# A rebuilt first block of a float32 transformer trunk on TensorE: new order, early fetches, other PSUM banks, and 17 matrix products on zeros

## The chip, the cores and the metric

One core of one Trainium2 chip. The metric is the device time of one launch in microseconds; lower is better.

## What is computed

A trunk of two layers over 256 tokens of width 2048, in float32. Layer 0 is sliding-window attention with grouped heads, layer 1 a chunked spatial gating unit, and each is followed by a squared-ReLU MLP of width 8192. The change lies in the very first piece, the keys and values of layer 0:

```python
a = rms_norm(h, g[0])                     # h = x, (1, 256, 2048)
qkv = h @ w_qkv                           # (2048, 2560): 2048 of q, 256 of k, 256 of v
k = qkv[..., Q_WIDTH:Q_WIDTH + KV_WIDTH]; v = qkv[..., Q_WIDTH + KV_WIDTH:]
q = partial_rotary(q, cos, sin); k = partial_rotary(k, cos, sin)
scores = jnp.einsum('bcqkgd,bcjkd->bckgqj', q, kb) * scale
```

## The kernel before

Every large product is cut into blocks of 512 output columns. A block needs 2048 rows of weight, which arrive in eight **slabs** of 512 KB (two times 128 rows). A slab lands in one of four slots of `w_raw`; ScalarE (ACT) rounds it to `w_hi`, and VectorE (DVE) makes `w_lo`, the remainder. TensorE (PE) then makes each float32 product as three: hi by hi, lo by hi, hi by lo (L357 to L359). One slab is six products for token tile 0 and six for token tile 1. `w_hi` and `w_lo` have eight slots each. SyncE (SP) issues the weight transfers in program order; the one into a slot waits until `lo_made` says that the slot's last slab has been split.

The left operand is made in **units**: four 128 x 128 pieces of the residual `h` (one of four column groups, one of two token tiles) are transposed on TensorE (L391), ACT writes `a_hi` from PSUM with the norm's gain (L650), DVE writes `a_lo` (L998). The list `UNIT` sets the order of the units.

Block 0 (`B_KV`) makes keys and values, block 1 (`B_Q`) the first 512 columns of the queries, and 83 more blocks follow. In `first_block(..., first_layer=True)` TensorE works through six slabs for token tile 0, six for tile 1, then the last two for each, with the transpositions of units 2 to 7 between. ACT also squares `h` in four pieces (L669) for the norm. `B_KV`'s results leave PSUM in `kv_evac` (L823, L826). DVE prepares the rotary angles (`rotary_angles`), ACT takes the sine, and DVE rotates the keys (L1209 to L1214). `transpose_k` (L553) on TensorE waits for these keys; it stands in `B_Q` behind 36 of that block's 96 products.

Nothing here is scheduled by a tool: each engine runs its own program in the written order, and semaphores tie them together.

Of the kernel before, what the change touches and what calls it, by code (L numbers as in the profile page):

```python
# [8 lines left out]
F32 = mybir.dt.float32  # L9
F32R = mybir.dt.float32r  # L10
I32 = mybir.dt.int32
ALU = mybir.AluOpType
# [3 lines left out]
P = 128  # L16
# [27 lines left out]
UNITS = len(UNIT)  # L44

# [43 lines left out]
def trunk(nc, x, positions, gains, w_qkv, w_o, sinks, w_in, ln_g, ln_b, w_s, b_s, w_out, w_up, w_down, out):  # L89
    ctx = ExitStack()  # L90
    with ctx:
# [58 lines left out]

        k_sb = yf[:, 0:1024].rearrange("p (t n) -> p t n", t=TOK)
# [23 lines left out]

        x_landed = [sem(f"x_landed{i}") for i in range(UNITS)]
# [7 lines left out]
        consts_made = sem("consts_made")  # L184
        hi_made = sem("hi_made")
# [61 lines left out]

        def slab_ahead(blk, i):

            i = i + 2 * LEAD  # L250
            return (blk, i) if i < 2 * PAIRS else (blk + 1, i - 2 * PAIRS)
# [3 lines left out]
        def _(sp):  # L255
            def load_x(n):
                pair, t = UNIT[n]
                f = slice(pair * COL, (pair + 1) * COL)
                sp.dma_start(h[:, t, f], x[0].rearrange("(t p) n -> p t n", p=P)[:, t, f]).then_inc(x_landed[n], 16)
# [20 lines left out]
            for units, slabs in (([0], (0, 2)), ([1], (2, 3)), ([2, 3], (3, 4)), ([4], (4, 6)), ([5, 6, 7], (6, 8))):  # L280
                for n in units:
                    load_x(n)
                load_block(B_KV, w_qkv[0], D, slabs=range(*slabs))
            with sp.Fori(0, NB) as j:
                load_block(j + B_Q, w_qkv[0], j * COL)
# [56 lines left out]
        def _(pe):  # L342
            def multiply_slab(blk, x_hi, x_lo, i, t):


                if i == 0:

                    at_least(pe, acc_free, blk * 2 + (t - 1))
# [3 lines left out]
                for k in range(SLAB_KB):  # L352
# [4 lines left out]
                    nc.tensor.matmul(acc[t][:, :], lhsT=x_hi[:, kb, tok], rhs=w1, start=(kb == 0), stop=False)  # L357
                    nc.tensor.matmul(acc[t][:, :], lhsT=x_hi[:, kb, tok], rhs=w2, start=False, stop=False)  # L358
                    last = nc.tensor.matmul(acc[t][:, :], lhsT=x_lo[:, kb, tok], rhs=w1,  # L359
# [21 lines left out]
            def transpose_unit(n, use0, first_layer=False):  # L381

                pair, t = UNIT[n]
# [24 lines left out]
            def first_block(blk, use0, first_layer=False):  # L408
# [5 lines left out]
                if first_layer:  # L414
                    transpose_unit(0, use0, True)
                    transpose_unit(1, use0, True)
                for step, (t, i) in enumerate(order):
# [3 lines left out]
                    if step in units:  # L421
                        transpose_unit(units[step], use0, first_layer)
                h_base[0] += 0 if first_layer else UNITS
# [118 lines left out]

            pe.wait_ge(consts_made, 2)
            pe.wait_ge(gains_landed, 16)
            nc.tensor.transpose(sc[0][:, 0:P], gain_rows[:, :], ident[:, :]).then_inc(small_filled, 1)


            first_block(B_KV, 0, first_layer=True)
# [75 lines left out]
        def _(act):  # L624
            def split_slab(blk, i):

                act.wait_ge(slab_landed[i % RAW_SLOTS],
                            blk * (32 * PAIRS // RAW_SLOTS) + 16 * (i // RAW_SLOTS + 1))
                at_least(act, slab_used, blk * (2 * PAIRS) + (i + 1 - SLOTS))
                nc.scalar.activation(w_hi[:, i % SLOTS, :], w_raw[:, i % RAW_SLOTS, :], ACT.Copy).then_inc(hi_made, 1)  # L630

            def split_slabs(blk, pair):
                for i in (2 * pair, 2 * pair + 1):
                    split_slab(blk, i)
# [9 lines left out]
            def split_unit(n, use0, norm):  # L644

                pair, t = UNIT[n]
# [18 lines left out]

            def square_h(t, part):
# [5 lines left out]
            def first_block(blk, use0, norm, evac, layer0=False):  # L672
# [3 lines left out]
                h_seen[0] += 0 if layer0 else UNITS  # L676

                def square(t, part):
                    if layer0:
                        for pair in (2 * part, 2 * part + 1):  # L680
                            act.wait_ge(x_landed[UNIT.index((pair, t))], 16)
                    else:

                        act.wait_ge(h_ready, h0 + UNIT.index((2 * part + 1, t)) + 1)
                    square_h(t, part)

                if layer0:
                    split_unit(0, use0, norm)
                    split_slabs(0, 0)
                    split_unit(1, use0, norm)  # L690
                    split_slabs(0, 1)
                split_unit(2, use0, norm)
                if layer0:
                    split_slabs(0, 2)
                else:
                    split_ahead(blk - 1, 3)
                split_unit(3, use0, norm)
                if layer0:
                    split_ahead(blk, 0)
                split_unit(4, use0, norm)  # L700
                if not layer0:
                    split_next(blk, 0)
                square(0, 0)
                split_unit(5, use0, norm)
                split_next(blk, 2 if layer0 else 1)
                square(1, 0)
                split_unit(6, use0, norm)
                split_next(blk, 3 if layer0 else 2)
# [3 lines left out]
                if not layer0:  # L712
                    split_next(blk, 3)
# [43 lines left out]
            def mlp(base, layer, use0, n, then):  # L757
# [42 lines left out]
                with act.Fori(1, QUARTERS - 1) as q:  # L800
# [8 lines left out]
            act.dma_start(pos_i[:, :], positions[0].rearrange("(t p) -> p t", p=P),  # L809
                          allow_slow_non_contiguous=True).then_inc(pos_landed, 16)  # L810
            for i in range(2):
                act.dma_start(sink_rows[i * CHUNK:(i + 1) * CHUNK, :, :],
                              sinks[0].rearrange("(a i e) -> i a e", i=2, e=2)[i].partition_broadcast(CHUNK),
                              allow_slow_non_contiguous=True).then_inc(sinks_landed, 16)
            act.wait_ge(small_filled, 1)
            nc.scalar.activation(gain_cols[:, :], sc[0][:, 0:P], ACT.Copy).then_inc(small_copied, 1)
# [3 lines left out]
            def kv_evac(t):  # L820
                product_done(act, B_KV, t)
                once = acc[t][:, 0:256].rearrange("p (g d) -> p g d", g=KVH)
# [3 lines left out]
                nc.scalar.activation(v_band[:, 2 * t, :], acc[t][:, 256:512], ACT.Copy, scale=r_in[:, t:t + 1]  # L826
                                     ).then_inc(acc_free, 1)

            first_block(B_KV, 0, 0, kv_evac, layer0=True)
# [139 lines left out]
        def _(dve):  # L969
# [4 lines left out]
            def split_slab(blk, i):  # L974

                dve.wait_ge(hi_made, blk * (2 * PAIRS) + (i + 1))
                nc.vector.tensor_tensor(w_lo[:, i % SLOTS, :], w_raw[:, i % RAW_SLOTS, :],  # L977
                                        w_hi[:, i % SLOTS, :].bitcast(F32), ALU.subtract).then_inc(lo_made, 1)

            def split_slabs(blk, pair):  # L980
                for i in (2 * pair, 2 * pair + 1):
                    split_slab(blk, i)
# [9 lines left out]
            def split_unit(n, use0, norm):  # L992
                pair, t = UNIT[n]
# [34 lines left out]
            def first_block(blk, use0, norm, layer0=False):  # L1028

                def update(n):  # L1030
                    if not layer0:
                        update_h(n)

                if layer0:
                    split_unit(0, use0, norm)
                    split_slabs(0, 0)
                    split_unit(1, use0, norm)
                    split_slabs(0, 1)
                split_unit(2, use0, norm)
                if layer0:  # L1040
                    split_slabs(0, 2)
                else:
                    split_ahead(blk - 1, 3)
                update(4)
                split_unit(3, use0, norm)
                if layer0:
                    split_ahead(blk, 0)
                update(5)
# [364 lines left out]
```

## Time and profile before

| | before |
|---|---|
| median of three runs | 1971.51 us (1971.41 to 1972.63) |
| profiled execution, its span | 1971.5 us |
| PE busy | 1949.2 us (99%) |
| DVE busy | 1076.2 us (55%) |
| ACT busy | 972.2 us (49%) |
| HBM read | 365.51 MB |

The span runs from the first to the last instruction; no time of the profiled execution is known beside it, so span and time are the same number here. Busy time is the sum of an engine's instructions without overlap. "PE" is a matrix product or a transposition, "PEld" its weight load.

### The profile page before, as it was taken

How to read it: one execution, taken by the hardware profiler on the slowest of the kernel's cores; microseconds unless marked ns; L12 is line 12 of the kernel's file. 1: busy time of each engine (PE TensorE's matmuls, PEld its weight loads, DVE VectorE, ACT ScalarE, POOL GpSimd, SP SyncE). 2: the span in 40 equal slices, each digit the busy share in tenths (PEclk: the TensorE clock that was granted, in tenths of full speed). 3: DMA queues.
4: the chain of work that ended last, by engine and by line, in shares of the span. 5: the costliest groups of instructions: out<-in, count | busy, mean ns of one | idle time of the engine just before them, and what ended most of it. 6: DMA issues, size and time to landing. Idle time of an engine off the chain costs nothing.

```text
span 1971.5 us, 26643 instructions
## 1 busy us (share of the span) xinstructions
PE 1949.2 (99%) x8914; PEld 1604.2 (81%) x8914; DVE 1076.2 (55%) x1276; ACT 972.2 (49%) x1339; POOL 6.2 (0%) x23
## 2 busy tenths in 40 slices
PE   7999999999999999999999999999999999999998
PEld 5777888888888888888888888888888888888886
DVE  5666575454454455455667655654544554544455
ACT  6666465435434543454564445654355435434542
POOL 0000000000000000000000000000000000000000
PEclk9999999999999999999999999999999999999999
DMA  6634656555555555555475555565555555555553
GB/s 205 203 128 164 207 197 203 191 192 182 191 195 180 189 192 192 192 172 196 150 259 171 192 189 177 173 212 199 194 177 188 196 191 190 178 199 189 182 192 107
DMA packets 189833, 368.40 MB, mean 187 GB/s; under 512 B 12616, under 2 KB 12752, under 8 KB 189008
## 3 DMA queue, kind: packets, MB, share of 16 engines
q1 hardware_dynamic: 187264, 360.75, 54.8%
q0 software_dynamic: 1040, 6.82, 0.9%
q8 instruction: 34, 0.56, 0.1%
q10 hardware_dynamic: 1472, 0.08, 0.0%
q14 instruction: 23, 0.19, 0.0%
HBM read 365.51 MB, written 2.10 MB: 186 GB/s over the span
## 4 chain that ended last, share of the span: by engine, by line
PE 98%; DMA 1%; ACT 0%; DVE 0%; SPq 0%; issue 0%; DVEq 0%; ACTq 0%
PE acc L357 31%; PE acc L359 31%; PE acc L358 31%; PE t L378 2%; DMA w_raw<-in_attn_w_qkv 1%; PE t L391 1%; PE scores L459 0%; PE o L481 0%; PE t L469 0%; PE scores L591 0%; PE t L439 0%; ACT a_hi L650 0%; DVE w_lo L977 0%; DVE h L1014 0%; ACT w_hi L630 0%
## 5 line engine op out<-in xcount | busy, mean ns | idle before, releaser
L977 DVE TENSOR_TENSOR w_lo<-w_raw,w_hi 128x1024 fp32r<-128x1024 f32 x680 | 820.6, 1224 | 632.1 <-ACT w_hi L630 603.5
L630 ACT ACTIVATE w_hi<-w_raw 128x1024 fp32r<-128x1024 f32 x680 | 708.4, 1058 | 626.0 <-PE acc L359 590.9
L357 PE MATMUL acc<-w_hi,a_hi 128*128 128x512 f32 x1440 | 573.5, 398 | 4.8 <-DVE w_lo L977 4.4
L359 PE MATMUL acc<-w_hi,a_lo 128*128 128x512 f32 x1440 | 563.2, 391 | 0.0
L358 PE MATMUL acc<-w_lo,a_hi 128*128 128x512 f32 x1440 | 562.5, 391 | 0.0
L357 PE MATMUL acc<-w_hi,b_hi 128*128 128x512 f32 x1280 | 500.9, 391 | 0.0
L359 PE MATMUL acc<-w_hi,b_lo 128*128 128x512 f32 x1280 | 498.4, 389 | 0.0
L358 PE MATMUL acc<-w_lo,b_hi 128*128 128x512 f32 x1280 | 498.1, 389 | 0.0
L357 PEld LDWEIGHTS acc<-w_hi,a_hi 128*128 128x128 f32 x1440 | 271.3, 188 | 62.2 <-issue 7.5
L359 PEld LDWEIGHTS acc<-w_hi,a_lo 128*128 128x128 f32 x1440 | 271.2, 188 | 58.3
L358 PEld LDWEIGHTS acc<-w_lo,a_hi 128*128 128x128 f32 x1440 | 271.6, 189 | 53.5
L357 PEld LDWEIGHTS acc<-w_hi,b_hi 128*128 128x128 f32 x1280 | 240.3, 188 | 50.3 <-issue 0.8
L359 PEld LDWEIGHTS acc<-w_hi,b_lo 128*128 128x128 f32 x1280 | 240.3, 188 | 50.3
L358 PEld LDWEIGHTS acc<-w_lo,b_hi 128*128 128x128 f32 x1280 | 240.4, 188 | 49.1
L726 ACT ACTIVATE s<-acc,r_in 128x512 f32<-128x512 f32 x80 | 55.1, 689 | 116.5 <-PE acc L359 115.8
L656 ACT ACTIVATE b_hi<-t 128x512 f32 (+1 forms) x72 | 42.9, 599 | 92.6 <-PE t L378 92.2
L1006 DVE TENSOR_TENSOR b_lo<-t,b_hi 128x512 f32 (+1 forms) x72 | 49.4, 688 | 65.6 <-ACT b_hi L656 65.6
L1075 DVE TENSOR_TENSOR y<-acc,y 128x512 f32 (+1 forms) x48 | 33.2, 691 | 69.7 <-PE acc L359 69.7
L733 ACT ACTIVATE o<-y 128x512 f32<-128x512 f32 (+1 forms) x32 | 19.3, 602 | 87.1 <-DVE y L1075 50.0
L998 DVE SCALAR_TENSOR_TENSOR a_lo<-t,gain_cols,a_hi 128x128 fp32r<-128x128 f32 x128 | 36.0, 344 | 21.8 <-ACT a_hi L650 21.4
L650 ACT ACTIVATE a_hi<-t,gain_cols 128x128 fp32r<-128x128 f32 x128 | 36.5, 370 | 19.6 <-PE t L391 18.8
L1077 DVE COPY y<-acc 128x512 f32 (+1 forms) x32 | 22.1, 691 | 41.0 <-PE acc L359 40.9
(120 smaller groups left out, 475.6 us busy)
## 6 DMA issues: line engine op xcount, KB each, us to landing
w_raw<-in_mlp_w_up SPq DMA_DIRECT2D x256, 512.0 KB, 4.2
w_raw<-in_mlp_w_down SPq DMA_DIRECT2D x256, 512.0 KB, 4.4
w_raw<-in_sgu_w_in SPq DMA_DIRECT2D x64, 512.0 KB, 4.6
w_raw<-in_attn_w_qkv SPq DMA_DIRECT2D x40, 512.0 KB, 4.6
w_raw<-in_attn_w_o SPq DMA_DIRECT2D x32, 512.0 KB, 4.2
w_raw<-in_sgu_w_out SPq DMA_DIRECT2D x32, 512.0 KB, 4.4
gain<-in_norm_gains POOLq DMA_DIRECT2D x4, 1024.0 KB, 5.4
h<-in_x SPq DMA_DIRECT2D x8, 256.0 KB, 11.4
```

The lines of the kernel that those rows point to most:

```text
L357: nc.tensor.matmul(acc[t][:, :], lhsT=x_hi[:, kb, tok], rhs=w1, start=(kb == 0), stop=False)
L358: nc.tensor.matmul(acc[t][:, :], lhsT=x_hi[:, kb, tok], rhs=w2, start=False, stop=False)
L359: last = nc.tensor.matmul(acc[t][:, :], lhsT=x_lo[:, kb, tok], rhs=w1, start=False, stop=(kb == KB - 1))
L378: last = nc.tensor.transpose(tb[t][:, k * P:(k + 1) * P], s[:, t, k * P:(k + 1) * P], ident[:, :])
L630: nc.scalar.activation(w_hi[:, i % SLOTS, :], w_raw[:, i % RAW_SLOTS, :], ACT.Copy).then_inc(hi_made, 1)
L650: last = nc.scalar.activation(a_hi[:, kb, t * P:(t + 1) * P], tb[n % 2][:, k * P:(k + 1) * P], ACT.Copy, scale=gain_cols[:, norm * KB + kb ...
L656: nc.scalar.activation(b_hi[:, bass.ds(kb0, 4), t * P:(t + 1) * P], tb[t][:, :].rearrange("p (k n) -> p k n", k=4), ACT.Copy).then_inc(t_h ...
L726: return nc.scalar.activation(dst, acc[t][:, :], func, scale=r_in[:, t:t + 1])
L977: nc.vector.tensor_tensor(w_lo[:, i % SLOTS, :], w_raw[:, i % RAW_SLOTS, :], w_hi[:, i % SLOTS, :].bitcast(F32), ALU.subtract).then_inc(lo ...
L998: nc.vector.scalar_tensor_tensor(out=a_lo[:, kb, tok], in0=tb[n % 2][:, k * P:(k + 1) * P], scalar=gain_cols[:, norm * KB + kb:norm * KB + ...
L1006: nc.vector.tensor_tensor(b_lo[at], tb[t][:, :].rearrange("p (k n) -> p k n", k=4), b_hi[at].bitcast(F32), ALU.subtract).then_inc(t_lo, 4)
L1075: nc.vector.tensor_tensor(dst, acc[t][:, :], dst, ALU.add).then_inc(acc_free, 1)
```

## The change

1. **Order of the transfers.** SP issues a unit of `x` and a slab in turn, eight of each (`X_UNIT` order: column group by column group, both token tiles). Slabs 4 to 7 of `B_KV` land in `y`, which is unused until then (`kv_raw`), so that none of the sixteen transfers waits for a slot. The first four slabs of `B_Q` are queued behind them, each behind the split of a `B_KV` slab.
2. **Order of the products.** `kv_block` replaces `first_block` for `B_KV`: two slabs for token tile 0, the same two for tile 1, then the next two. ACT and DVE split unit i and slab i in turn, then `B_Q`'s slabs.
3. **Banks.** `B_KV` accumulates in the two banks of `scores`, not in `acc`, so `B_Q` starts without waiting for `kv_evac`.
4. **Products on zeros.** DVE zeroes a part of `b_hi`; TensorE multiplies it 17 times into the bank `o1`, which nothing reads: five of 512 columns first of all, four of 256 after unit 0, four of 512 and four of 256 after unit 1.
5. **Small transfers.** The positions and the sinks (ACT's queue, rows of 4 and 8 bytes) are issued behind the eighth split instead of at the start. `neg_sink` moves behind the rotation of the first queries.

```diff
+X_UNIT = [(pair, t) for pair in range(NB) for t in range(TOK)]
+        kv_raw = yf[:, :].rearrange("p (i n) -> p i n", i=RAW_SLOTS)
-            for units, slabs in (([0], (0, 2)), ([1], (2, 3)), ([2, 3], (3, 4)), ([4], (4, 6)), ([5, 6, 7], (6, 8))):
...
+            for i in range(2 * PAIRS):
+                load_x(i)
+                sp.dma_start(raw(B_KV, i).rearrange("p (k n) -> p k n", k=SLAB_KB), kv_source(i)
+                             ).then_inc(slab_landed[i] if i < RAW_SLOTS else kv_landed[i - RAW_SLOTS], 16)
+            for i in range(RAW_SLOTS):
+                sp.wait_ge(lo_made, i + 1)
...
-                if i == 0:
-
-                    at_least(pe, acc_free, blk * 2 + (t - 1))
+                if i == 0 and not (isinstance(blk, int) and blk <= B_Q):
+
+                    pe.wait_ge(acc_free, blk * 2 + (t - 1))
...
+            def idle_products(count, n):
+
+                zeros = b_hi[:, 0:2, :].rearrange("p k n -> p (k n)")
+                for _ in range(count):
+                    nc.tensor.matmul(ob[1][:, 0:n], lhsT=zeros[:, 0:P], rhs=zeros[:, 0:n], start=True, stop=True)
+
+            def kv_block():
+
+                transpose_unit(0, 0, True)
+                idle_products(4, SEQ)
+                transpose_unit(1, 0, True)
+                idle_products(4, SEQ * TOK)
+                idle_products(4, SEQ)
+                for pair in range(PAIRS):
+                    for t in range(TOK):
+                        for i in (2 * pair, 2 * pair + 1):
+                            pe.wait_ge(t_lo, X_UNIT.index((pair, t)) * 4 + (i % 2 + 1) * SLAB_KB)
+                            multiply_slab(B_KV, a_hi, a_lo, i, t, sc)
+                            if pair < PAIRS - 1 and (t, i % 2) in ((0, 1), (1, 0)):
+                                transpose_unit(2 * pair + 2 + t, 0, True)
...
+            pe.wait_ge(zeros_made, 1)
+            idle_products(5, SEQ * TOK)
             pe.wait_ge(consts_made, 2)
             pe.wait_ge(gains_landed, 16)
...
+            def kv_block(evac):
+
+                squares = {3: (0, 0), 4: (1, 0), 6: (0, 1), 7: (1, 1)}
+                for i in range(2 * PAIRS):
+                    split_unit(i, 0, 0, X_UNIT)
+                    split_slab(B_KV, i)
+                    if i in squares:
+                        t, part = squares[i]
+                        for pair in (2 * part, 2 * part + 1):
+                            act.wait_ge(x_landed[X_UNIT.index((pair, t))], 16)
+                        square_h(t, part)
+                load_positions()
+                load_sinks()
+                split_next(B_KV, 2, 3, 4)
+                take_root()
+                split_next(B_KV, 5)
+                act.wait_ge(norm_done, norms[0])
+                evac(0)
+                evac(1)
+                split_next(B_KV, 6, 7)
...
+            def kv_block():
+
+                for i in range(2 * PAIRS):
+                    split_unit(i, 0, 0, X_UNIT)
+                    split_slab(B_KV, i)
+                split_next(B_KV, 2, 3)
+                input_norm()
+                split_next(B_KV, 4, 5)
+                rotary_angles()
+                split_next(B_KV, 6, 7)
...
+            nc.vector.memset(b_hi[:, 0:2, :].bitcast(F32), 0.0).then_inc(zeros_made, 1)
```

`split_next(B_KV, i)` splits the slab six ahead, so `split_next(B_KV, 2)` is the first slab of `B_Q`, and 3 to 7 are its slabs 1 to 5.

On TensorE the program began, before the change, with the transposition of the gains, then units 0 and 1 and at once the products:

```order
L545 MATMUL scores<-ident,gain_rows 128x128 [waits gains_landed,consts_made]
L391 MATMUL t<-ident,h 128x128 [waits x_landed0]
...
L391 MATMUL t<-ident,h 128x128 [waits x_landed1]
...
L357 MATMUL acc<-w_hi,a_hi 128x512 [waits lo_made,t_lo]
L358 MATMUL acc<-w_lo,a_hi 128x512
```

It now begins so (`o` is the bank that nothing reads):

```order
L431 MATMUL o<-b_hi 128x512 [waits zeros_made]
L431 MATMUL o<-b_hi 128x512 x4
L584 MATMUL o<-ident,gain_rows 128x128 [waits gains_landed,consts_made]
L410 MATMUL t<-ident,h 128x128 [waits x_landed0]
L410 MATMUL t<-ident,h 128x128 x3
L431 MATMUL o<-b_hi 128x256 x4
L410 MATMUL t<-ident,h 128x128 [waits x_landed1]
L410 MATMUL t<-ident,h 128x128 x3
L431 MATMUL o<-b_hi 128x512 x4
L431 MATMUL o<-b_hi 128x256 x4
L376 MATMUL scores<-w_hi,a_hi 128x512 [waits lo_made,t_lo]
```

The products on zeros stand around the first two units, ahead of the first real product.

On ACT, at the end of the unit splits (`a_hi`), the order before was this, with two of `B_Q`'s slabs split between the squares (`b_hi,pre_ssq`), and the positions and sinks long issued:

```order
L630 ACTIVATE w_hi<-w_raw 128x1024 [waits slab_used,slab_landed1]
L669 ACTIVATE b_hi,pre_ssq<-h 128x1024 [waits x_landed6,x_landed2]
...
L669 ACTIVATE b_hi,pre_ssq<-h 128x1024 [waits x_landed7,x_landed5]
L662 ACTIVATE root<-mean_sq 128x2 [waits norm_mean]
L823 ACTIVATE y<-acc,r_in 128x512 [waits half_done,norm_done]
L826 ACTIVATE work<-acc,r_in 128x256
L630 ACTIVATE w_hi<-w_raw 128x1024 [waits slab_used,slab_landed2]
```

And now, from the last slab of `B_KV` (which comes out of `y`) on:

```order
L675 ACTIVATE w_hi<-y 128x1024
L720 ACTIVATE b_hi,pre_ssq<-h 128x1024
L708 DMA pos_i<-in_positions 128x2x1
L713 DMA sink_rows<-in_attn_sinks 64x8x2 x2
L675 ACTIVATE w_hi<-w_raw 128x1024 x3
L703 ACTIVATE root<-mean_sq 128x2
L675 ACTIVATE w_hi<-w_raw 128x1024
L872 ACTIVATE y<-scores,r_in 128x512
L875 ACTIVATE work<-scores,r_in 128x256
```

The three small transfers and all of `B_Q`'s splits now stand behind the last square.

On DVE the rotary angles (`pos_f` to `red`) stood ahead of `B_Q`'s slabs 2 to 5 (`w_lo` x4), and then came the rotation of the keys:

```order
L1026 RECIPROCAL r_in<-root 128x2
L1176 CAST pos_f<-pos_i 128x2
...
L1192 TENSOR_SCALAR red<-red 128x16
L1193 TENSOR_SCALAR red<-red 128x32
L1196 TENSOR_SCALAR neg_sink<-sink_rows 128x16
L977 TENSOR_TENSOR w_lo<-w_raw,w_hi 128x1024 x4
L1209 TENSOR_TENSOR rot<-y,sincos 128x128
```

Now two of these slabs stand between the norm and the angles, and two between the angles and the rotation:

```order
L1077 TENSOR_TENSOR sum_sq<-pre_ssq 128x2 [waits norm_sum]
...
L1071 RECIPROCAL r_in<-root 128x2 [waits norm_root]
L1026 TENSOR_TENSOR w_lo<-w_raw,w_hi 128x1024 [waits hi_made] x2
L1218 CAST pos_f<-pos_i 128x2 [waits consts_made,pos_landed]
...
L1235 TENSOR_SCALAR red<-red 128x32 [waits dve_chain]
L1026 TENSOR_TENSOR w_lo<-w_raw,w_hi 128x1024 [waits hi_made] x2
L1249 TENSOR_TENSOR rot<-y,sincos 128x128 [waits qkv_evac,sincos_made]
```

## Rows read from the trace of the kernel before

**Rows 1.** Windows, 566 to 1166 us: busy us (and instructions) of each engine, clock, DMA share, GB/s.

```profile
566.00:1166.00 600.00, 599.74 (x2709) 496.00 (x2709) 333.23 (x365) 285.99 (x349) 1.98 (x3) 1.00 0.57 189
```

**Rows 2.** Timeline, 0 to 11 us: start, duration, engine, and idle time with its end.

```profile
1.52 0.45 ACTq L809 DMA_DIRECT2D pos_i<-in_positions  x1
...
2.74 0.73 ACTq L812 DMA_DIRECT2D sink_rows<-in_attn_sinks  x1
...
4.39 1.06 PE L391 MATMUL t<-ident,h 128*128 128x128 f32 x4
...
5.56 1.14 ACT L650 ACTIVATE a_hi<-t,gain_cols 128x128 fp32r<-128x128 f32 x4 [0.64 <-PE t L391]
...
7.86 1.22 DVE L977 TENSOR_TENSOR w_lo<-w_raw,w_hi 128x1024 fp32r<-128x1024 f32 x1
...
10.46 1.11 PE L391 MATMUL t<-ident,h 128*128 128x128 f32 x4 [5.01 <-DMA h<-in_x]
```

**Rows 3.** DMA, 8 to 12, 20 to 24, 16 to 20 us: packets, MB, share; time to landing.

```profile
q1 hardware_dynamic: 384, 0.73, 53.8%
q10 hardware_dynamic: 391, 0.00, 4.5%
...
q1 hardware_dynamic: 786, 1.46, 95.6%
...
w_raw<-in_attn_w_qkv SPq DMA_DIRECT2D x1, 512.0 KB, 9.6
```

**Rows 4.** Timeline at two gaps of TensorE; windows, one microsecond in the second gap.

```profile
14.89 0.66 PE L391 MATMUL t<-ident,h 128*128 128x128 f32 x4 [0.76 <-DMA h<-in_x]
...
23.16 0.77 PE L357 MATMUL acc<-w_hi,a_hi 128*128 128x512 f32 x1 [4.40 <-DVE w_lo L977]
...
22.00:23.00 1.00, 0.00 (x0) 0.00 (x0) 1.00 (x2) 1.00 (x5) 0.00 (x0) 0.50 1.04 393
```

**Rows 5.** Timeline, one unit and one slab on their way through three engines.

```profile
31.54 0.60 PE L391 MATMUL t<-ident,h 128*128 128x128 f32 x4
...
32.17 1.14 ACT L650 ACTIVATE a_hi<-t,gain_cols 128x128 fp32r<-128x128 f32 x4 [0.66 <-PE t L391]
...
33.19 1.07 ACT L630 ACTIVATE w_hi<-w_raw 128x1024 fp32r<-128x1024 f32 x1
...
33.35 1.13 DVE L998 SCALAR_TENSOR_TENSOR a_lo<-t,gain_cols,a_hi 128x128 fp32r<-128x128 f32 x4 [1.60 <-ACT a_hi L650]
...
34.14 1.07 ACT L669 ACTIVATE b_hi<-h 128x1024 fp32r<-128x1024 f32 x1
...
34.39 1.22 DVE L977 TENSOR_TENSOR w_lo<-w_raw,w_hi 128x1024 fp32r<-128x1024 f32 x1
...
34.75 0.60 PE L391 MATMUL t<-ident,h 128*128 128x128 f32 x4
...
35.38 0.88 ACT L650 ACTIVATE a_hi<-t,gain_cols 128x128 fp32r<-128x128 f32 x3
```

**Rows 6.** Timeline, 40 to 54 us: norm, angles, rotation, and the transposition of the keys.

```profile
40.80 0.15 DVE L1063 TENSOR_TENSOR sum_sq<-pre_ssq 128x2 f32<-128x2 f32 x1
...
41.51 0.17 DVE L1176 CAST pos_f<-pos_i 128x2 f32<-128x2 int32 x1
...
43.19 0.39 PE L357 MATMUL acc<-w_hi,a_hi 128*128 128x512 f32 x1
...
43.93 0.18 DVE L1193 TENSOR_SCALAR red<-red 128x32 f32<-128x32 f32 x1
...
50.13 0.29 DVE L1209 TENSOR_TENSOR rot<-y,sincos 128x128 f32<-128x128 f32 x1
...
51.27 0.28 DVE L1214 TENSOR_TENSOR y<-rot 128x128 f32<-128x128 f32 x1
...
53.16 0.39 PE L359 MATMUL acc<-w_hi,a_lo 128*128 128x512 f32 x1
53.40 0.60 PE L553 MATMUL t<-ident,y 128*128 128x128 f32 x4
```

More of the change, by code:

```diff
@@ L173, in trunk @@
         junk = ob[1]
+        kv_landed = [sem(f"kv_landed{i}") for i in range(RAW_SLOTS)]
         x_landed = [sem(f"x_landed{i}") for i in range(UNITS)]
@@ L256, in load_x @@
             def load_x(n):
-                pair, t = UNIT[n]
+                pair, t = X_UNIT[n]
                 f = slice(pair * COL, (pair + 1) * COL)
@@ L277, in load_mlp, with kv_source @@
                             load_block(q * (2 * NB) + j + (base + NB), w_down[layer], j * COL, q * KB)
-            for units, slabs in (([0], (0, 2)), ([1], (2, 3)), ([2, 3], (3, 4)), ([4], (4, 6)), ([5, 6, 7], (6, 8))):
[L281 to L284, printed above, removed]
+            def kv_source(i):
+                rows = w_qkv[0].rearrange("(k p) n -> p k n", p=P)
+                return rows[:, i * SLAB_KB:(i + 1) * SLAB_KB, D:D + COL]
+            for i in range(2 * PAIRS):
[4 more added lines that the diff above has]
+                sp.wait_ge(lo_made, i + 1)
+                src = w_qkv[0].rearrange("(k p) n -> p k n", p=P)[:, i * SLAB_KB:(i + 1) * SLAB_KB, 0:COL]
+                sp.dma_start(w_raw[:, i, :].rearrange("p (k n) -> p k n", k=SLAB_KB), src).then_inc(slab_landed[i], 16)
+            load_block(B_Q, w_qkv[0], 0, slabs=range(RAW_SLOTS, 2 * PAIRS))
+            with sp.Fori(1, NB) as j:
                 load_block(j + B_Q, w_qkv[0], j * COL)
@@ L642, in split_ahead, with split_unit @@
                 split_next(blk, 2 * pair, 2 * pair + 1)
-            def split_unit(n, use0, norm):
-                pair, t = UNIT[n]
+            def split_unit(n, use0, norm, order=UNIT):
+                pair, t = order[n]
                 act.wait_ge(t_filled, use0 + n + 1)
@@ L664, in _, with load_positions, load_sinks @@
             norms = [0]
+            def load_positions():
+                act.dma_start(pos_i[:, :], positions[0].rearrange("(t p) -> p t", p=P),
+                              allow_slow_non_contiguous=True).then_inc(pos_landed, 16)
+            def load_sinks():
+                for i in range(2):
+                    act.dma_start(sink_rows[i * CHUNK:(i + 1) * CHUNK, :, :],
+                                  sinks[0].rearrange("(a i e) -> i a e", i=2, e=2)[i].partition_broadcast(CHUNK),
+                                  allow_slow_non_contiguous=True).then_inc(sinks_landed, 16)
             def square_h(t, part):
@@ L675, in first_block @@
+            def first_block(blk, use0, norm, evac):
                 h0 = h_seen[0]
-                h_seen[0] += 0 if layer0 else UNITS
+                h_seen[0] += UNITS
                 def square(t, part):
[L679 to L684, printed above, removed]
-                    square_h(t, part)
@@ L808, in _ @@
             nc.scalar.activation(warm[:, :], ident[:, 0:1], ACT.Sqrt)
[L809 to L814, printed above, removed]
             act.wait_ge(small_filled, 1)
-            nc.scalar.activation(gain_cols[:, :], sc[0][:, 0:P], ACT.Copy).then_inc(small_copied, 1)
+            nc.scalar.activation(gain_cols[:, :], ob[0][:, 0:P], ACT.Copy).then_inc(small_copied, 1)
             act.wait_ge(small_copied, 1)
@@ L990, in split_ahead, with split_unit @@
                 split_next(blk, 2 * pair, 2 * pair + 1)
-            def split_unit(n, use0, norm):
-                pair, t = UNIT[n]
+            def split_unit(n, use0, norm, order=UNIT):
+                pair, t = order[n]
                 dve.wait_ge(t_hi, use0 + n + 1)
```

136 lines of the change are left out of this document (55 added, 81 removed).

## The prediction

> **What bounds the kernel.** I read the page first (PE busy for 99% of the span, DVE for 55%, ACT for 49%), then the busy time by stretch: in the middle of the program PE is busy for 599.74 of 600 us [rows 1]. TensorE's waits lie at the two ends, most of them in the first 24 us, and there I read the timeline. So TensorE sets the time, and a change of the first block is worth exactly what it moves a TensorE instruction behind which nothing waits any more. The best such mark is the transposition of the keys, `transpose_k`: it starts at 53.40 us, 0.24 us behind the product ahead of it, without a wait [rows 6]. The program behind it does not change. My measure of the change is therefore when `transpose_k` starts.
>
> Three things are lost before it. TensorE waits 5.01 us for `x`; the second unit's transposition starts at 10.46 us [rows 2]. From 18.76 to 23.16, 4.40 us, it waits for the split of slab 3, and in this wait the granted clock falls to 0.50, which is 1.2 GHz [rows 4]. The products behind it run at that level for about five microseconds.
>
> The cause of the late `x` and slab 3 is in the DMA queues. From 8 to 12 us queue q1 (x and weights) moves 384 packets, and q10 (gains, positions, sinks) 391 packets that hold next to nothing; from 20 to 24 us, with q10 all but empty, q1 moves 786 [rows 3]. The sum is the same, about 195 packets a microsecond: a packet of 4 bytes takes the turn of one of 2 KB. While they are under way the weights get half of the rate, 183 instead of 366 GB/s.
>
> **The early fetches.** A unit of `x` is 128 packets, a slab 256. The second unit now stands behind 384 packets, plus 128 of the gains: 640 in all, at 195 a microsecond 3.3 us, from about 2.3 us on. With 0.5 to 1 us until the last has landed that is 6.1 to 6.6 us, not 10.46. All sixteen transfers are 3072 packets, 16 us, so slab 7 has landed by about 19 us. The recurrence below asks for it at 34 us: the DMA leaves the path.
>
> **The new block as a chain.** What it costs comes from one unit and slab on their way through the engines [rows 5]. From the start of a transposition it is 0.63 us to `a_hi`, 1.18 more to `a_lo`, 1.04 more to `w_lo`, 1.22 until that is done, and 0.14 to the product: 4.21 us. Products follow each other at (53.16 - 43.19)/44 = 0.2266 us [rows 6], so six are 1.36. Transpositions of two units are 3.21 us apart with twelve products between [rows 5]; that leaves 0.49 us for a transposition.
>
> In `kv_block` the unit of the next pair is transposed behind the second slab of token tile 0. Until the next pair's first slab is needed TensorE has 2 x (0.49 + 1.36) = 3.70 us of work, but the chain takes 4.21: it waits 0.5. The second slab's `w_lo` comes 2.2 us after the first's (DVE does a slab, 1.14, then a unit, 1.04), and TensorE has six products, 1.36, to fill this: it waits 0.85. A pair takes 4.21 + 2.2 + 1.36 = 7.8 us instead of the 6.4 of its work. A square on ACT takes 1.24 us (34.14 to 35.38) [rows 5]. The one at i = 3 falls in a gap of ACT. Those at i = 4 and i = 6 stand between the slab and the next unit and push the second `w_lo` back by 1.0 us.
>
> Start: DVE's first `w_lo` begins at 7.86 us as before [rows 2]; then unit 1, and `w_lo` of slab 1 ends at 7.86 + 1.14 + 1.04 + 1.22 = 11.26. That needs unit 1 transposed from 6.6 us on, which the landing above just gives. Products of slab 1 start at 11.4, the transposition of unit 2 at 12.8, of unit 4 at 12.8 + 7.8 = 20.6, of unit 6 at 20.6 + 8.8 = 29.4. The block ends 4.21 + 2.2 + 1.0 us and eighteen products (4.08) later: **40.9 us**. Before it ended 36 products ahead of 53.40, at 45.2. So the block alone gives 4.3 us.
>
> **What is late next.** The splits of `B_Q` and the keys' rotation. ACT ends slab 7 at 29.4 + 5.8 = 35.2 us and the last square at 36.4. Then come the three small DMA issues, as long as before: from 1.52 to 3.47, 1.95 us [rows 2]. So `B_Q`'s slab 0 is rounded from 38.4 us on, where before ACT had two of these slabs done before 38. DVE then works without a pause: slabs 0 and 1 end at 41.9, the norm takes 0.8 (from `sum_sq` at 40.80 to 41.59) [rows 6], slabs 2 and 3 end at 45.0, the angles take 2.6 (41.51 to 44.11) [rows 6] to 47.6, slabs 4 and 5 end at 50.0, and the rotation takes 1.42 (50.13 to 51.55) [rows 6] to 51.4. ACT is beside this, not ahead: `kv_evac` of tile 1 ends by 45.3, slabs 4 and 5 by 47.6, table and sine by 49.2.
>
> TensorE would reach `transpose_k` at 40.9 + 36 x 0.2266 = 49.0 us. The keys are rotated at 51.4, so it starts at **51.5** and waits 2.5 us. Against 53.40 that is 1.9 us gained; 2.4 of the 4.3 are given back. Of the 1.9 nothing is lost later: ACT and DVE are half idle in the rest [rows 1].
>
> **Edits at no cost.** Products on zeros: five of 512 columns at 1.2 GHz are 2.1 us and end at about 3.5 us, before the gains' transposition (right ahead of unit 0, which starts at 4.39) [rows 2]. The eight between unit 1 and the first product end by 10.1 us even at 1.2 GHz, and the chain asks for slab 1 at 11.4; six real products lie between, so at worst TensorE is 0.1 to 1.2 us late. The zeroing itself is one DVE instruction in an idle stretch. Bound from below: nothing; from above, with the clock at 1.2 GHz until 12 us, 1.0 us. I take nothing, since the longer activity should have raised the clock by 9 us: before, the engine was at work without a long pause from 10.46 us on [rows 2], and at 14.89 a transposition takes 0.66 us instead of 1.11 [rows 4]. The other banks: `B_Q` would wait for `kv_evac` of tile 0 (44.2 us in the new order), so without them the block's gain would be gone; with them it costs nothing. `neg_sink` is 0.17 us of DVE.
>
> **The small transfers** now meet `B_Q`'s slabs 4 to 7. They are issued at 36.4 to 38.4 us; `B_Q`'s slabs 4 and 5 are requested when slabs 0 and 1 are split, 40.8 and 42.0. Those 512 packets at half of the rate [rows 3] take 5.2 us, and land at about 47.7. DVE can't use slab 5 before 48.8, so ACT must have it by 47.6. Cost: 0 to 0.2 us; if the rate is three quarters of this, 1.9 us. I add 0.1, and forecast 1971.5 - 1.9 + 0.1 = 1969.7 us. The profiled span equals the median of the runs (1971.51), so it needs no correction.
>
> **Rivals.** 0.2% (3.9 us) is about what a measurement of this kernel can tell from no change.
> - *`transpose_k` is not late (16%).* If the ACT and DVE chain is 2.5 us shorter than I make it, for instance since squares and splits overlap better, the whole 4.3 us stay: 1967.2, and up to 1966.5 with faster pairs. For it: ACT and DVE are not full in the rows. Against it: DVE has no gap from 39.5 to 51.4 us in my sum.
> - *The small packets hold `B_Q` up (12%), slower.* Slab 5 lands late. Each microsecond of its landing past 47.6 is one at `transpose_k`; past 49.5 the kernel is slower than before. A landing 9.6 us after the request (a slab took this before, beside such packets [rows 3]) gives 51.6, `transpose_k` at 55.4, and 1973.5.
> - *The clock stays low (9%), slower.* The block now waits at every pair, up to 1.9 us at a time. With all its products at 0.427 us (1.2 GHz) the chain becomes product bound and `transpose_k` moves to about 58.5: 1976.6. Before, the wait of 4.40 us cost the clock, and one of 0.76 us did not [rows 4]; 1.9 lies between. By the Trainium skill, "TensorE: Matmul & The Clock Gate", section "HAM oscillation — how this bites in real kernels", a kernel whose bursts are short beside its DMA waits falls back to the low clock at every tile; taken for this block that is the 1976.6. In the trace above the shorter wait speaks against it.
> - *It does little (6%).* If `x` lands at 9 us, because the rate and not the order was the limit, all is 1.9 to 2.4 us later: 1971.5 to 1972.
>
> **Chances.** My forecast, `transpose_k` between 50.5 and 52.8 us, 57%. Its own range is 1968.6 to 1971.0. The range for 8 in 10 takes in the first rival and the middle of the second: 1966.9 to 1973.5. Faster by over 0.2%: the first rival and a corner of the forecast, 17%. Slower: the clock and the far end of the packets, 10%. Within: 73%.
>
> **What would show it.** Unit 1's transposition at 6.1 to 6.6 us; unit 2's at 12.8, unit 4's at 20.6, unit 6's at 29.4; TensorE idle 0.5 and 0.9 us in the second pair, 0.5 and 1.9 in the third and fourth; granted clock 1.00 from 9 us on. `B_KV`'s last product near 40.9; a wait of about 2.5 us of the keys' transposition for DVE, starting at 51.5; q1 at some 98 packets a microsecond while q10 runs, now from 38 to 50 us. Wrong would be: a low clock behind 12 us, ACT waiting for a `B_Q` slab past 48 us, or a new wait of TensorE behind 55 us.

## The result and the profile after

The changed kernel takes 1974.64 us (median of 20 runs, 1972.83 to 1976.51), the kernel before 1972.05 us (20 runs, 1971.1 to 1973.09). The ratio is 1.0013, with a 95% interval of 1.0007 to 1.0019: **2.6 us slower**, where 1969.7 was forecast. The time lies outside the range. The difference is small, 0.13%, but its interval does not reach zero, and it goes the other way than I forecast.

The chain of the rebuilt block came out as worked out; what follows it did not. TensorE's timeline of the changed kernel (start, duration, and the idle time ahead with its end) has the forecast marks 12.8, 20.6 and 29.4 at 12.84, 20.67 and 29.37. `B_Q` starts at 40.80:

```profile
1.47 2.50 PE L431 MATMUL o<-b_hi 128*128 128x512 f32 x5 [1.47 <-DVE b_hi L1239]
...
6.60 0.66 PE L410 MATMUL t<-ident,h 128*128 128x128 f32 x4 [0.31 <-DMA h<-in_x]
...
12.84 0.60 PE L410 MATMUL t<-ident,h 128*128 128x128 f32 x4
...
20.67 0.60 PE L410 MATMUL t<-ident,h 128*128 128x128 f32 x4
...
27.90 0.47 PE L376 MATMUL scores<-w_hi,a_hi 128*128 128x512 f32 x1 [1.38 <-DVE w_lo L1026]
...
29.37 0.60 PE L410 MATMUL t<-ident,h 128*128 128x128 f32 x4
...
40.80 0.39 PE L376 MATMUL acc<-w_hi,a_hi 128*128 128x512 f32 x1
...
52.88 0.66 PE L592 MATMUL t<-ident,y 128*128 128x128 f32 x4 [3.76 <-DVE y L1254]
...
57.71 0.60 PE L592 MATMUL t<-ident,y 128*128 128x128 f32 x4
```

Against [rows 6]: `transpose_k` starts at 52.88 instead of 53.40, behind a wait of 3.76 us where there was none. Its two halves are 4.83 us apart; in the kernel before they are 3.2. Each of the two has a cause of its own.

The first is seen on ACT, in its timeline (an ACTq line is the issue of a transfer). It rounds `B_Q`'s slabs 0 to 2 from 35.99 us on and is done with `kv_evac` by 42.8. Then it stands still:

```profile
31.96 0.39 ACTq L708 DMA_DIRECT2D pos_i<-in_positions  x1
...
33.11 0.65 ACTq L713 DMA_DIRECT2D sink_rows<-in_attn_sinks  x1
...
34.96 1.10 ACT L720 ACTIVATE b_hi<-h 128x1024 fp32r<-128x1024 f32 x1
...
35.99 2.99 ACT L675 ACTIVATE w_hi<-w_raw 128x1024 fp32r<-128x1024 f32 x3
...
47.48 1.06 ACT L675 ACTIVATE w_hi<-w_raw 128x1024 fp32r<-128x1024 f32 x1 [4.65 <-DMA w_raw<-in_attn_w_qkv]
48.76 1.06 ACT L675 ACTIVATE w_hi<-w_raw 128x1024 fp32r<-128x1024 f32 x1 [0.23 <-DMA w_raw<-in_attn_w_qkv]
...
51.13 0.23 ACT L882 ACTIVATE sincos<-red 128x32 f32<-128x32 f32 x1
```

The two at 47.48 and 48.76 us are `B_Q`'s slabs 4 and 5, requested from 38.4 us on. The DMA view from 36 to 40 us (first two lines) and from 40 to 44 shows what the queues did meanwhile: packets, MB, share, then time to landing.

```profile
q10 hardware_dynamic: 441, 0.00, 4.9%
...
w_raw<-in_attn_w_qkv SPq DMA_DIRECT2D x2, 512.0 KB, 9.2
...
q1 hardware_dynamic: 57, 0.12, 8.4%
q10 hardware_dynamic: 322, 0.00, 3.6%
```

The small packets went at 110 a microsecond although they had the DMA engines to themselves (which were busy for 4.9% of the time), and they did not share: the weights requested at 38.4 us moved no packet before 43 us and 57 until 44 us. The two slabs took 9.2 us.

The second cause is the clock. The windows view (busy us of PE, PEld, DVE, ACT and POOL, then PEclk, DMA share, GB/s) shows it at full level when the wait ends at 52.88 us, at half from 55 us on at the latest, and back by 58 us:

```profile
52.00:53.00 1.00, 0.12 (x1) 0.12 (x2) 0.96 (x5) 1.00 (x2) 0.00 (x0) 1.00 1.01 391
...
55.00:56.00 1.00, 1.00 (x4) 0.81 (x3) 0.92 (x4) 0.08 (x1) 0.00 (x0) 0.50 0.69 121
...
58.00:59.00 1.00, 1.00 (x7) 0.87 (x6) 0.24 (x1) 0.60 (x1) 0.00 (x0) 1.00 1.03 373
```

### The profile page after: what moved, and what is told of

The parts are those of the page before. It is cut to its first block, busy times and chain, and to the rows that moved or that the text cites. A ratio compares the mean times of both kernels' runs of the same rounds, so it can differ in the third digit from the quotient of the medians.

```text
span 1972.5 us, 26652 instructions
## 1 busy us (share of the span) xinstructions
PE 1953.3 (99%) x8931; PEld 1605.5 (81%) x8931; DVE 1075.9 (55%) x1277; ACT 971.5 (49%) x1339; POOL 6.2 (0%) x23
## 4 chain that ended last, share of the span: by engine, by line
PE 97%; DVE 1%; ACT 1%; DMA 1%; issue 0%; ACTq 0%; DVEq 0%
PE acc L376 31%; PE acc L378 31%; PE acc L377 31%; PE t L397 2%; PE t L410 1%; ACT a_hi L691 1%; PE scores L496 0%; DVE w_lo L1026 0%; DMA w_raw<-in_attn_w_qkv 0%; PE o L518 0%; DVE a_lo L1043 0%; PE t L506 0%; PE scores L630 0%; ACT b_hi L720 0%; ACT w_hi L675 0%
## 5 line engine op out<-in xcount | busy, mean ns | idle before, releaser
L376 PE MATMUL acc<-w_hi,a_hi 128*128 128x512 f32 x1408 | 559.5, 397 | 0.4 <-ACT y L781 0.2
L378 PE MATMUL acc<-w_hi,a_lo 128*128 128x512 f32 x1408 | 549.9, 391 | 0.0
L377 PE MATMUL acc<-w_lo,a_hi 128*128 128x512 f32 x1408 | 549.2, 390 | 0.0
L378 PEld LDWEIGHTS acc<-w_hi,a_lo 128*128 128x128 f32 x1408 | 264.7, 188 | 56.7
L376 PEld LDWEIGHTS acc<-w_hi,a_hi 128*128 128x128 f32 x1408 | 264.7, 188 | 56.5 <-issue 2.9
L377 PEld LDWEIGHTS acc<-w_lo,a_hi 128*128 128x128 f32 x1408 | 265.1, 188 | 52.4
```

The lines of the kernel that those rows point to most:

```text
L376: nc.tensor.matmul(bank[t][:, :], lhsT=x_hi[:, kb, tok], rhs=w1, start=(kb == 0), stop=False)
L377: nc.tensor.matmul(bank[t][:, :], lhsT=x_hi[:, kb, tok], rhs=w2, start=False, stop=False)
L378: last = nc.tensor.matmul(bank[t][:, :], lhsT=x_lo[:, kb, tok], rhs=w1, start=False, stop=(kb == KB - 1))
```

## The experiments

Each kernel was run beside the kernel before on the same chip. Ratios are to it. The kernel before has medians of 1971.98 to 1972.72 us in these rounds, so a difference between two kernels of different rounds is good to some tenths of a microsecond; the marks of the profiled runs stand beside it. Twelve kernels:

| kernel | median us | ratio (95%) | `transpose_k` at |
|---|---|---|---|
| e0_before | 1972.63 | 1.0002 (0.9993 to 1.0011) | 52.7 |
| e1_small_in_gap | 1968.90 | 0.9983 (0.9974 to 0.9992) | 49.55 |
| e2_fill_wait | 1973.03 | 1.0005 (0.9996 to 1.0014) | 53.16 |
| e3_sink_rows | 1969.02 | 0.9985 (0.9976 to 0.9994) | 48.90 |
| e4_before_sink_rows | 1964.82 | 0.9964 (0.9950 to 0.9978) | 44.98 |
| e5_no_zeros | 1971.00 | 0.9994 (0.9985 to 1.0004) | 49.91 |
| e6_acc_banks | 1970.31 | 0.9990 (0.9981 to 0.9999) | 50.5 |
| e7_slot_waits | 1969.08 | 0.9986 (0.9977 to 0.9995) | 48.77 |
| e8_best | 1964.71 | 0.9960 (0.9946 to 0.9973) | 45.54 |
| e9_units_early | 1963.46 | 0.9955 (0.9942 to 0.9969) | 43.4 |
| e10_x_early | 1964.54 | 0.9960 (0.9947 to 0.9974) | 44.7 |
| e11_units_small | 1969.95 | 0.9988 (0.9979 to 0.9997) | 48.90 |

### The yardstick

e0_before is the kernel before.

> The kernel before once more, unchanged, as a yardstick: its span beside its time, and its spread. The changed kernel's profiled span is 1.0 us above that of before (1972.5 against 1971.5), but its median time is 2.6 us above. Theory A (what lies outside the span is the same for both): the span here varies and is near 1970.2 us, with the time 1.8 us above it, as for the changed kernel. Theory B (the change also costs time outside the span): span 1971.5, time within 0.6 us of it.

Its profiled execution took 1972.63 us with a span of 1970.8, and in all its runs the time is the span and 1.8 us; so it is for the changed kernel (1974.34 and 1972.5). Theory A holds. By the same 1.8 us, the span of 1971.5 that the prediction started from belongs to one of that kernel's longer executions, of about 1973.3 us.

### The small packets: elsewhere, or fewer

e1_small_in_gap issues them behind slab 4:

```diff
                         square_h(t, part)
-                load_positions()
-                load_sinks()
+                    if i == 4:
+                        load_positions()
+                        load_sinks()
```

> The changed kernel, with positions and sinks issued behind the split of slab 4 (near 22 us) instead of behind slab 7; their 1280 small packets at 110 a microsecond then end by 36 us, before B_Q's slab 4 is requested at 38.4. Theory M (the packets hold the weights back): slab 4 lands in 4.6 us, not 9.2, the keys are rotated at 48.8, transpose_k starts at 49.0 without a wait, the clock stays up; 5.5 us less than the changed kernel, 3 to 4.4 us less than before. Rival R (ACT's and DVE's own order is what makes the keys late): transpose_k still at 51.5 or later with a wait of 2.5 us or more; at most 1.5 us less than the changed kernel. Rival R2: the small packets now hold back B_Q's slabs 0 to 3, and ACT waits for slab 0 past 36 us.

e3_sink_rows fetches the whole row of 32 sinks to every partition, and DVE picks:

```diff
-                for i in range(2):
-                    act.dma_start(sink_rows[i * CHUNK:(i + 1) * CHUNK, :, :],
-                                  sinks[0].rearrange("(a i e) -> i a e", i=2, e=2)[i].partition_broadcast(CHUNK), ...)
+                act.dma_start(sink_rows[:, :, :, :].rearrange("p a i e -> p (a i e)"),
+                              sinks[0].partition_broadcast(P)).then_inc(sinks_landed, 16)
```

> The changed kernel, with the sinks fetched as 128 rows of 128 bytes instead of 1024 pieces of 8 bytes, and one more small DVE instruction to pick each half's entries; place of issue unchanged. Theory M (the number of packets counts): the small transfers end by 36 us, transpose_k starts at 49.0 without a wait, 5.5 us less than the changed kernel. Rival R (ACT's and DVE's order): transpose_k at 51.5 or later. Rival R3 (the place among the weights counts, not the number): slab 4 still lands 9 us after its request.

In both, the wait of `transpose_k` is gone, and the time is 5.7 and 5.6 us under the changed kernel's 1974.64. The lines of e3_sink_rows that answer to those above are, first from its DMA view (36 to 40 us):

```profile
w_raw<-in_attn_w_qkv SPq DMA_DIRECT2D x2, 512.0 KB, 4.1
```

and from its timeline, ACT's two lines and TensorE's one:

```profile
42.67 1.07 ACT L675 ACTIVATE w_hi<-w_raw 128x1024 fp32r<-128x1024 f32 x1
44.13 1.06 ACT L675 ACTIVATE w_hi<-w_raw 128x1024 fp32r<-128x1024 f32 x1 [0.39 <-DMA w_raw<-in_attn_w_qkv]
...
48.90 0.60 PE L592 MATMUL t<-ident,y 128*128 128x128 f32 x4
```

The same two slabs now take 4.1 us, and the keys are ready in time. Theory M holds: the sinks' 1024 pieces held the weights back. (The new fetch has fewer pieces and longer ones, 16 KB in all instead of 8, so these two runs do not tell the number from the length.) Rival R (DVE's and ACT's order), which was a step of my prediction, falls. R3 falls too, since the place of issue was the same. R2 did not come about: in e1 ACT rounds `B_Q`'s slab 0 from 36.58 us without a wait. For e1 the mark is 0.5 us later than expected: its whole block runs 0.6 us late from the start.

### The clock alone

e2_fill_wait puts 16 unread products into the wait.

```diff
-            plain_block(B_Q, a_hi, a_lo, {(1, 0): [lambda: transpose_k(0)], ...
+            plain_block(B_Q, a_hi, a_lo, {(1, 0): [lambda: idle_products(16, SEQ * TOK), lambda: transpose_k(0)], ...
```

> The changed kernel, with 16 more unread products of 512 columns right ahead of transpose_k, where TensorE waits 3.8 us. Theory M: transpose_k stays at 52.9 us, but the granted clock stays 1.00, the two groups of key transpositions are 3.2 us apart instead of 4.8, and the kernel is 1.6 us faster than the changed one (about 1 us slower than before). Rival (the clock falls for another reason, such as the low activity since 16 us): it falls all the same, and nothing is won or 16 products at 0.427 us make transpose_k later.

TensorE's timeline of this kernel:

```profile
49.22 3.79 PE L431 MATMUL o<-b_hi 128*128 128x512 f32 x16
53.16 0.66 PE L592 MATMUL t<-ident,y 128*128 128x128 f32 x4
...
56.41 0.60 PE L592 MATMUL t<-ident,y 128*128 128x128 f32 x4
```

The granted clock stays 1.00, the halves are 3.25 us apart, and the kernel is 1.6 us under the changed one (1974.64 - 1973.03). The wait itself made the clock fall, and that is 1.6 us of the loss. With the 4.0 us at `transpose_k` (52.88 against 48.90 in e3) it makes up the 5.6 us between the changed kernel and e3.

### The old block with the same small fix

e4_before_sink_rows is the kernel before with the sinks' fetch of e3 and nothing else.

> The kernel before, with nothing changed but the fetch of the sinks: 128 rows of 128 bytes instead of 1024 pieces of 8 bytes, and one more small DVE instruction. Theory M (the small packets, not the order of the old block, made x and slab 3 late): the small packets end by about 7 us, slab 3 lands near 14 us instead of 20.6, the 4.4 us wait and the low clock behind it go, and transpose_k starts 3 to 6 us earlier than in the kernel before: at least 0.15% less than before, as good as the rebuilt block. Rival (the rebuilt order is what brings the gain): less than 1 us gained.

It is 0.36% faster than the kernel before and beats every version with the change's own order of units. TensorE's timeline, to be held against [rows 2, 4, 6]:

```profile
9.21 1.12 PE L391 MATMUL t<-ident,h 128*128 128x128 f32 x4 [3.68 <-DMA h<-in_x]
...
16.71 0.60 PE L391 MATMUL t<-ident,h 128*128 128x128 f32 x4
...
19.93 0.60 PE L391 MATMUL t<-ident,h 128*128 128x128 f32 x4
...
23.14 0.60 PE L391 MATMUL t<-ident,h 128*128 128x128 f32 x4
...
44.98 0.60 PE L553 MATMUL t<-ident,y 128*128 128x128 f32 x4
```

Behind 9.21 us TensorE waits for nothing until 60 us, and from 16.71 us on the units are 3.2 us apart, which is twelve products and a transposition. From 8 to 12 us q1 moves 845 packets here, against 384 in [rows 3]. The old order was good; its fetch of the sinks was not. And this is what the rebuilt block is worth by itself: with the sinks as rows in both kernels it is 4.2 us slower than the old one (1969.02 against 1964.82, `transpose_k` at 48.90 against 44.98). It waits for `w_lo` at every pair, 4.5 us in all from 12 us on, where the old block does not wait.

### The other parts of the change, each on e3_sink_rows

e5_no_zeros leaves out the 17 products on zeros:

```diff
                 transpose_unit(0, 0, True)
-                idle_products(4, SEQ)
                 transpose_unit(1, 0, True)
-                idle_products(4, SEQ * TOK)
-                idle_products(4, SEQ)
...
-            idle_products(5, SEQ * TOK)
```

> The changed kernel with the sinks as rows (e3_sink_rows), without the 17 products on zeros. If they hold the clock up: the products from 9.2 us on run at 1.2 GHz for some microseconds, the two first slabs take 2.56 us each instead of 1.4, unit 2's transposition starts 1.0 to 1.5 us later than 12.8, and all behind it too: 1.0 to 1.5 us slower than e3_sink_rows. Rival (the wait for slab 1's split covers it, or the clock would be up anyway): within 0.3 us of e3_sink_rows.

```profile
9.29 0.76 PE L376 MATMUL scores<-w_hi,a_hi 128*128 128x512 f32 x1 [1.44 <-DVE w_lo L1020]
9.85 0.63 PE L377 MATMUL scores<-w_lo,a_hi 128*128 128x512 f32 x1
...
12.83 0.39 PE L378 MATMUL scores<-w_hi,a_lo 128*128 128x512 f32 x1
```

In its profiled execution the first products, from 9.29 us, are about 0.43 us apart until 12.8, which is the pace of 1.2 GHz, and `transpose_k` is 1.0 us later. (PEclk reads 1.00 in these microseconds; so early in the program the pace has to be read.) The median is 2.0 us above e3. The zeros are worth 1 to 2 us.

e6_acc_banks takes the banks `acc` again:

```diff
-                            multiply_slab(B_KV, a_hi, a_lo, i, t, sc)
+                            multiply_slab(B_KV, a_hi, a_lo, i, t)
```

> The changed kernel with the sinks as rows, with B_KV accumulated in the banks acc again, so that B_Q's first product waits for kv_evac of tile 0, which ends near 41.8 us, where TensorE is ready at 40.7. Theory (the banks are worth this wait): TensorE waits 1.1 us there, transpose_k at 50.0 instead of 48.9, 1.1 us slower than e3_sink_rows. Rival (evacuation is on time): no difference.

```profile
42.21 0.50 PE L376 MATMUL acc<-w_hi,a_hi 128*128 128x512 f32 x1 [0.97 <-ACT work L873]
```

This row of its timeline is `B_Q`'s first product: it waits 0.97 us for the evacuation. The kernel is 1.3 us slower than e3.

e7_slot_waits makes SP wait for the split of slab i - 4 ahead of slab i:

```diff
                 load_x(i)
+                if i >= RAW_SLOTS:
+                    sp.wait_ge(lo_made, i - RAW_SLOTS + 1)
```

> The changed kernel with the sinks as rows, where SP waits for the split of slab i - 4 before it issues slab i of B_KV, as it would with four slots only. Theory (the early fetch of slabs 4 to 7 is worth nothing once the queue is free and the order is right): slab 4 is requested near 9 us, slab 7 near 19 and needed at 34, no wait moves, within 0.3 us of e3_sink_rows. Rival (the early fetches carry the gain): TensorE waits for slabs 4 to 7, over 1 us slower than e3_sink_rows.

It takes 1969.08 us, 0.06 us from e3: fetching slabs 4 to 7 early, into `y`, is worth nothing once the queue is free.

### The chain inside the block

e9_units_early, again on e3_sink_rows, transposes each unit one group of six products earlier:

```diff
-                            if pair < PAIRS - 1 and (t, i % 2) in ((0, 1), (1, 0)):
-                                transpose_unit(2 * pair + 2 + t, 0, True)
+                            if pair < PAIRS - 1 and t == 0:
+                                transpose_unit(2 * pair + 2 + i % 2, 0, True)
```

> The changed kernel with the sinks as rows, with both units of the next column group transposed one product group earlier (behind slab 2p and slab 2p+1 of token tile 0). Theory C (the chain unit, a_hi, a_lo, w_lo paces the rebuilt block: TensorE waits for it 0.4 to 1.4 us per slab, 4.5 us in all from 12 us on): the waits shrink by 1.4 us each, the block ends about 3 us earlier, transpose_k near 46, 3 us less than e3_sink_rows. Rival (ACT and DVE are full, so earlier units only make them finish the slabs in another order): less than 1 us.

The waits view shows what TensorE waited for `w_lo` until 60 us, in the changed kernel (first line) and in this one:

```profile
PE scores L376 <- DVE w_lo L1026: 5.6, 8, 1.4
```

```profile
PE scores L376 <- DVE w_lo L1024: 0.6, 3, 0.2
```

Theory C holds, and the gain was underestimated: 5.6 us (1969.02 - 1963.46) instead of 3. I had taken only the shift of a transposition; in fact the chain no longer adds up from pair to pair. This is the fastest kernel, 0.45% under the kernel before.

e10_x_early and e8_best go on from e4. In e10 the second unit of `x` is requested ahead of slab 1, since e4 still waits 3.68 us for it; e8 has the 17 products on zeros besides.

```diff
-            for units, slabs in (([0], (0, 2)), ([1], (2, 3)), ...
+            for units, slabs in (([0], (0, 1)), ([1], (1, 3)), ...
```

> The kernel before with the sinks as rows (e4_before_sink_rows), with the second unit of x moved ahead of slab 1 in SP's order. Theory: unit 1 lands near 6.7 us instead of 9.2, the first products start when w_lo of slab 0 is ready, near 9.2 instead of 10.1, and the rest follows: 0.5 to 1 us less than e4_before_sink_rows. Rival: slab 2 and 3 then set the pace, no difference.

> As e10_x_early, plus the 17 products on zeros of the change. If clock and fetch order add up: all real products at 2.4 GHz from 9.2 us on, 1 to 2.5 us less than e4_before_sink_rows (1962.3 to 1963.8 against a kernel before of 1972), the fastest version so far. Rival: DVE's splits of slabs 2 and 3 take over as the bound, at most 0.5 us less than e10_x_early.

Neither gains what was expected. e10 (1964.54, five runs, 1964.38 to 1964.95) overlaps with e4 (1964.56 to 1965.19). Its first product starts 0.5 us earlier and its fourth unit 1.0 us (15.68 against 16.71), but `transpose_k` only 0.3 us. It waits 1.42 us for slab 0's `w_lo`, as expected, and 0.51 us at 18.17 us for slab 4's. Ahead of that one ACT had waited 1.03 us for slab 3 to land, which fits the rival in part; it is not tested. In e8's profiled execution TensorE gets `x` only at 8.68 us, and the zeros leave a gap of 2.34 us. The clock falls at about 10 us, 1.3 us behind the gap's end, with the products on zeros running (the last line is of the windows view):

```profile
8.68 0.66 PE L392 MATMUL t<-ident,h 128*128 128x128 f32 x4 [2.34 <-DMA h<-in_x]
...
11.01 0.63 PE L358 MATMUL acc<-w_hi,a_hi 128*128 128x512 f32 x1
...
10.00:11.00 1.00, 1.00 (x6) 0.90 (x5) 0.00 (x0) 0.67 (x1) 0.00 (x0) 0.52 1.06 408
```

### A second case for the packets

e11_units_small is e9's order with the change's own small transfers.

> The changed kernel with the units transposed earlier (as in e9_units_early) but with its own small transfers, 1280 packets, issued now near 27 us. A test of the packet account on a case it was not made from: 1280 packets at 110 a microsecond end near 39 us; B_Q's slabs 4 and 5, requested near 33 and 34, land near 41 and 42.3, about 9 us after their request; sine, rotation, and transpose_k at 46.2 to 46.8, where e9_units_early has it at 43.4; TensorE waits about 3 us and the clock may fall behind it. 3 to 5 us slower than e9_units_early, 6 us less than the changed kernel. Rival (the packets only delay what the rebuilt chain had made late anyway): within 1 us of e9_units_early.

```profile
48.90 1.11 PE L592 MATMUL t<-ident,y 128*128 128x128 f32 x4 [5.25 <-DVE y L1254]
```

The direction holds, the rival (within 1 us of e9) falls, and the size is above the forecast: slab 4 is rounded from 43.50 us on, not 41, and `transpose_k` waits 5.25 us. Behind that wait the clock is low, and the two halves are 5.13 us apart. The kernel is 6.5 us slower than e9. It is 4.7 us, not 6, under the changed one. The block now ends earlier, so the transfers are issued earlier too (26.95 instead of 31.96), but the slabs are asked for 5.5 us earlier too (32.90 instead of 38.37). A faster block only waits longer for the same packets.

## Why the prediction was wrong

- **The chain of the block: right.** Four marks within 0.1 us, and unit 1 was transposed from 6.60 us; the 0.5 to 1 us that its forecast allowed for the landing stood in no row.
- **"What is late next": wrong in its cause.** I made DVE and ACT the bound of the rotation (51.4 us) and put the three DMA issues on ACT's path with 1.95 us. They did not stand there: they were issued from 31.96 us on, 3.0 us before the square began that stands ahead of them in the program (34.96), and `B_Q`'s slab 0 began at 35.99 instead of 38.4. With the packets gone the keys were ready at 48.5 and nothing waited (e3). So my first rival, `transpose_k` not late, was the truth about ACT and DVE.
- **"The small transfers": the step that failed.** My sum has them at 0.1 us; they cost 4.0 us at `transpose_k` and, through the clock, 1.6 more. I let the weights take half of the rate beside the small packets and landed slab 5 at about 47.7, although requested as late as 42.0. The [rows 3] count, 384 against 391, shows sharing between transfers that had all been requested by then. It does not say what a weight requested behind 1280 small packets gets. It got nothing until they were nearly done, and alone they ran at 110 a microsecond, not 195. Nor was it the time of the DMA engines that the small packets took: in [rows 3] the two queues had them busy for 53.8% and 4.5%. Slab 5 was taken at 48.8. That is my second rival, at 1.2 us past its bound of 47.6. That `transpose_k` came only 1.3 us behind its forecast (52.88 against 51.6) is luck: without the packets ACT and DVE let it start at 48.90 (e3), 2.6 us earlier than the 51.5 I made it, and that hid most of the 4.0 us.
- **The clock: the rival's mechanism, in another place.** The waits in the block, up to 1.39 us, did not lower the clock. The wait that the packets made did: 1.6 us (e2). I had priced the two rivals apart, and one was the cause of the other. By the Trainium skill, "TensorE: Matmul & The Clock Gate", section "HAM oscillation — how this bites in real kernels", a long enough DMA wait between bursts of products drops the clock, so that the next burst starts slow. This trace agrees in part: behind the one long wait (3.76 us) PEclk is 0.50 from 55 us on, but still 1.00 in the first microsecond of products. That the short waits at every pair would do the same was my reading, and they did not.
- **"The profiled span equals the median, so it needs no correction": wrong.** The time is 1.8 us above the span in every run. The starting point, 53.40 and 1971.5, was one of the longer executions; another had `transpose_k` at 52.74 and 1970.8. From there to the changed kernel's 1972.5 is 1.7 us: 0.1 at `transpose_k` and 1.6 of clock. So the 4.6 us between my 1969.7 and the profiled execution's 1974.34 are 1.8 of this, 1.3 at `transpose_k` and 1.6 of clock, to 0.1 us. The first is an error of the starting number alone; the direction was wrong by the other two.
- **The zeros and the banks.** Zeros at no cost: right; e5 shows what they save. "Without the banks the block's gain would be gone": too much, it is 1.3 us (e6), since `kv_evac` of tile 0 ends at 41.9 us, not at 44.2. Early fetches: they left the path as said, but the slots would have done (e7).

Where the expected gain went, in marks of the profiled runs: the rebuilt block ends 3.8 us before the old one in e0 (52.74 - 36 x 0.2266 = 44.6 against 40.8); 3.9 us go to the wait behind the small packets and 1.6 to the clock. But those 3.8 us were gained on a block that its own small packets held up; on the block without them the new order gains nothing (e4). The changed kernel's 20 times form two groups, 1974.2 to 1974.7 (with one at 1972.8 below) and 1975.3 to 1976.5, the second, but for one run, at a mean clock of 0.997 instead of 0.998. That fits a low clock of varying length (in e11 the halves are 5.13 us apart, here 4.83), but only one execution was profiled, so it stays open.

## What to carry to other kernels

Look at the pieces of a transfer, not at its bytes: 8 KB of sinks in 1024 pieces held back two slabs, 1 MB of weights, and fetching the sinks as whole rows was worth 7.2 us. Rebuilding the block around them lost 2.6 us, and even its best order (e9) is only some 1.4 us ahead of the old block with that one fetch mended. Moving such a transfer later does not make it cheaper; look which request will stand behind it in its new place, and what waits for that. And price a wait of TensorE with the clock behind it: here a wait of 3.76 us cost 1.6 us more, waits of up to 1.39 us cost no clock, and what lies between was seen once only (2.34 us in e8, low behind it).

## What was not expected of the hardware

- The sinks' packets of 8 bytes move at 107 to 110 a microsecond with nothing beside them (441 in 4 us), while the weights' and `x`'s packets of 2 KB move at 204 to 211 (815 and 845 in 4 us of e4). A weight transfer requested behind the small ones took 9.2 to 10.6 us, against 4.1 with 128 rows in their place. How the queues decide this was not tried.
- It is not small packets as such: the 256 of the positions, of 4 bytes, passed in about 1 us. This is the changed kernel's DMA view from 33 to 34 us, the first line, and from 34 to 35 us, when only the sinks' were left. What makes the sinks' slow stays open.

```profile
q10 hardware_dynamic: 286, 0.00, 13.9%
...
q10 hardware_dynamic: 107, 0.00, 4.7%
```

- A DMA issue of ACT does not stand behind ACT's arithmetic that is still to come: the positions were issued at 31.96 us, while the last square, which stands ahead of them in the program, began at 34.96. In e1 the issue came at 22.01 and the square ahead of it at 23.85.
- The products on zeros can miss their aim: behind a gap of 2.34 us the clock was low (e8). Behind the waits of up to 1.39 us in the block of the changed kernel it was not.
